# Two layers of a streaming encoder on one core: the sixteen products of o(t) in another order

## The reference, cut to what matters

```python
def step(S, inp):
    qb, kb, vb, gb = (t.astype(f32) for t in inp)
    b = jnp.cumsum(gb, axis=1)
    inter = jnp.einsum('bthk,bhkv->bthv', qb * jnp.exp(b), S)
    decay = jnp.exp(jnp.where(causal, b[:, :, None] - b[:, None, :], -jnp.inf))
    att = jnp.einsum('bthk,bshk,btshk->bhts', qb, kb, decay)
    intra = jnp.einsum('bhts,bshv->bthv', att, vb)
    b_end = b[:, -1]
    S_new = jnp.exp(b_end)[..., None] * S + jnp.einsum(
        'bshk,bshv->bhkv', kb * jnp.exp(b_end[:, None] - b), vb)
    return S_new, inter + intra
```

## Time and profile before

| | |
|---|---|
| median of 3 runs | 2413.31 us (2410.1 to 2415.28) |
| the profiled execution | 2407.27 us |
| its span, first to last instruction | 2405.3 us |
| TensorE busy in the span | 2186.8 us (91%) |
| mean granted TensorE clock | 0.939 of full speed |
| TensorE's share of the chain that ended last | 27% of the pieces the page prints |
| L1083 and L1085 in that chain | 1.3% each |

### The profile page before, as it was taken

The page is one execution under the profiler, slowest core; times in us unless marked ns, Lnnn a source line. Parts: engine busy times, 40 slices in busy tenths (PEclk is TensorE's granted clock), DMA queues, the critical chain, the costliest instruction groups (busy, mean ns, idle before and its releaser), DMA issues. The chain is left out here.

```text
span 2405.3 us, 27372 instructions
## 1 busy us (share of the span) xinstructions
PE 2186.8 (91%) x9906; PEld 1331.1 (55%) x9930; DVE 1484.6 (62%) x3125; ACT 643.1 (27%) x1478; POOL 328.1 (14%) x418
## 2 busy tenths in 40 slices
PE   4999999997999968889959999999989999789887
PEld 3544444466777755545445444444667677545554
DVE  3357999995545454654333589999955454564651
ACT  3333001113333323232143420010133333233331
POOL 0000000000000043543200000000000001353541
PEclk9999999998999968998979999999989999698988
DMA  7111322213022020221051113222120220111211
GB/s 276 63 65 62 114 73 72 66 39 69 12 81 76 1 96 22 90 87 62 36 174 49 64 67 110 72 76 66 42 62 7 82 75 31 66 64 49 97 53 55
DMA packets 144006, 169.95 MB, mean 71 GB/s; under 512 B 68560, under 2 KB 106192, under 8 KB 143600
## 3 DMA queue, kind: packets, MB, share of 16 engines
q1 hardware_dynamic: 118400, 135.52, 17.6%
q10 hardware_dynamic: 25472, 32.66, 3.8%
HBM read 115.53 MB, written 62.50 MB: 74 GB/s over the span
## 5 line engine op out<-in xcount | busy, mean ns | idle before, releaser
L767 PE MATMUL ps<-wring,xnT_arena 128*128 128x512 f32 (+3 forms) x2304 | 883.0, 540 | 0.0
L767 PEld LDWEIGHTS ps<-wring,xnT_arena 128*128 128x128 f32 x2304 | 430.7, 190 | 431.4 <-issue 369.4
L1483 DVE TENSOR_SCALAR_CACHE_REDUCE arena<-arena,theta 32x1056 bf16<-32x1056 f32 x496 | 471.6, 987 | 8.8
L1065 PE MATMUL ps<-arena 128*128 128x128 f32 (+1 forms) x632 | 134.4, 343 | 100.2 <-DVE arena L1671 84.3
L1571 DVE TENSOR_REDUCE small<-ps 128x1 f32<-128x192 f32 (+9 forms) x148 | 114.1, 771 | 154.9 <-PE ps L942 148.3
L1065 PEld LDWEIGHTS ps<-arena 128*128 128x128 f32 x632 | 103.1, 213 | 188.6 <-DVE arena L1671 142.8
L1009 PE MATMUL ps<-wring,arena 128*128 128x512 f32 x320 | 172.8, 662 | 5.7 <-DVE arena L1612 5.7
L1176 ACT COPY arena<-ps 128x512 f32<-128x512 f32 (+2 forms) x96 | 51.2, 533 | 464.4 <-PE ps L767 464.4
L1468 DVE SCALAR_TENSOR_TENSOR arena<-arena,iw 128x512 f32<-128x512 f32 (+6 forms) x224 | 135.7, 606 | 57.3 <-ACT arena L1231 50.4
L1324 ACT ACTIVATE arena<-ps,small 128x192 f32<-128x192 f32 (+9 forms) x148 | 111.0, 750 | 159.5 <-DVE small L1571 159.4
L1009 PE MATMUL ps<-wring,xnT_arena 128*128 128x512 f32 x256 | 135.1, 652 | 0.0
(11 more groups left out here) (239 smaller groups left out, 2670.7 us busy)
## 6 DMA issues: line engine op xcount, KB each, us to landing
wring<-in_w_in SPq DMA_DIRECT2D x24, 1024.0 KB, 7.7
projected<-arena ACTq DMA_DIRECT2D x96, 256.0 KB, 2.0
arena<-residual SPq DMA_DIRECT2D x36, 512.0 KB, 5.6
arena<-projected SPq DMA_DIRECT2D x36, 384.0 KB, 3.8
arena<-projected SPq DMA_DIRECT2D x18, 512.0 KB, 5.9
residual<-arena SPq DMA_DIRECT2D x18, 512.0 KB, 2.7
wring<-in_w_out SPq DMA_DIRECT2D x8, 1024.0 KB, 6.5
out<-arena SPq DMA_DIRECT2D x16, 512.0 KB, 3.9
```

The source lines that it names most:

```text
L767: o = mm(bank(pbank(k), 0, wide), xnT[:, c, t * P:(t + 1) * P], w, start=(c == 0), stop=(c == CH - 1))
L1065: o = mm(bank(level_bank(k), 2 * n_ * g, 2 * n_), keys[:, g * P:(g + 1) * P], queries[:, :, g, :], start=True, stop=True)
L1483: V.tensor_scalar(cmp_out[r, (i % 2) * WMAX:(i % 2) * WMAX + uw[u]], score[u][r], th_, 0.0, op, ALU.add, accum_out=into[r, i:i + 1]).then_ ...
```

## The change

The products and their addresses stay the same, sixteen in each tile. Before, each head's attention product was followed by its state product. Now all eight attention products come first, then all eight state products. Among these, even and odd heads alternate, so that the weights' rows alternate between 0 to 63 and 64 to 127, and the output between banks 6 and 7. Before, each attention product had `start=True`, the flag with which a product overwrites. Now the flag stands on the first product into each bank alone (m = 0, h = 0 and 1); the other attention products have `start=False`.

```diff
-                        for m, att, vv, qb, st in ((0, attA, la[:, 2, :], QbA, s_hgrn), (1, attD, ld[:, 2, :], QbD, s_ret)):
+                        sides = ((0, attA, la[:, 2, :], QbA, s_hgrn), (1, attD, ld[:, 2, :], QbD, s_ret))
+                        n_ = NS if t == 0 else P
+                        for m, att, vv, qb, st in sides:
+                            for h in range(H):
+                                oc = (6 + h % 2) * 512 + P * m + HD * (h // 2)
+                                mm(ps[:, oc:oc + HD], att[:, h, :], vv[:, HD * h:HD * h + HD], start=(m == 0 and h < 2), stop=False, skip_group_check=True)
+                        for m, att, vv, qb, st in sides:
                             for h in range(H):
                                 a, b = hp(h)
                                 oc = (6 + h % 2) * 512 + P * m + HD * (h // 2)
-                                o = mm(ps[:, oc:oc + HD], att[:, h, :], vv[:, HD * h:HD * h + HD], start=True, stop=False, skip_group_check=True)
-                                n_ = NS if t == 0 else P
                                 o = mm(ps[0:n_, oc:oc + HD], qb[a:b, (h // 2) * P:(h // 2) * P + n_], st[a:b, 0 if t == 0 else 1, h // 2, :],
-                                       start=False, stop=True, skip_group_check=True)
+                                       start=False, stop=(m == 1 and h >= 2), skip_group_check=True)
                         o.then_inc(x_o, 1)
```

## The result

| | before | changed |
|---|---|---|
| median of the runs (4 each) | 2412.91 us (2410.1 to 2415.28) | 2311.99 us (2307.53 to 2312.84) |
| the profiled execution | 2407.27 us | 2312.26 us |
| its span | 2405.3 us | 2310.3 us |
| mean granted TensorE clock | 0.939 | 0.957 |

The changed kernel takes 0.9585 of the time before (95% interval 0.9568 to 0.9601): 100.9 us less by the medians. Forecast were 2314.7 us, and 98.6 us less. A later set of runs of the changed kernel, on another chip, gave 0.9584 (0.9557 to 0.9612; label r_changed).

A forecast was written before the change was run, and what follows sets the result against it. TensorE, waiting for nobody in tile 2, was taken as the bound. Savings of 70.9 + 11.7 + 6.0 + 10 = 98.6 us from 2413.3 gave a median of 2314.7 us; 8-in-10 range 2300 to 2350 us.

The forecast's parts named there:

- o(t) at full clock, 2.98 us: o(t): attention run 1.80 us, state products 0.90, and a change of weights at 0.14 after each.
- the rate of L979: Attention products in o(t): sixteen records in one run at the softmax stage's spacing, 0.1125 us each, 1.80 us.
- L819's strips: State products in o(t): row halves run two at a time, as four 32-row strips ran together; 0.90 us.
- Rival (c): o(t)'s attention records: same-row weight loads don't overlap running products, 3.12 us for 1.80, kernel 2338 us; chance 0.03.
- The clock: Tiles 2 to 8: TensorE's granted clock holds at 1.00 from o(t) to the next L1030, against mean 0.77.
- rival (a): Tiles 2 to 8: the clock falls all the same, 6.7 us at half clock each; 46 saved, 2367 us; chance 0.12.
- Tiles 2 to 7: Stretch from o(t) to the next L1030: 8.74 us against 14.65, 5.91 saved, twelve times, 70.9 us.
- Tile 8: Stretch from o(t) with 32 records of L1009: 17.34 us against 23.25, saved in two layers, 11.7 us.
- Tile 0: Stretch from o(t) stays at half clock: 5.78 us against 8.76, 3.0 saved, twice, 6.0 us.
- Tile 1: Stretch from o(t), clock uncertain: between 2.0 and 7.5 us saved; the middle taken, 5 each, 10 in all.
- What is late next: L1009 behind o(t) also waits for `x_zr`, ready 3.45 us after o(t)'s first record; TensorE gets there after 3.58.
- one more spell of half clock between the levels in some tiles: Levels between tiles: possible extra half clock, counted only in the forecast's own upper limit of 2325 us.

The follow-up runs named there:

- e7: Kernel before, with three added dense 128x512 products, result unused, in each o(t) from tile 1 on; 2406.52 us, ratio 0.9971.
- e3: Kernel before, reordered to two attention products, then their two state products, four times over, flags as before; 2331.45 us, ratio 0.9683.
- e9: Changed kernel with the odd heads' state products taken from rows 0 to 63 too, so no upper half; 2337.21 us.
- e1: Changed kernel with state products of all even heads first, then all odd heads, so neighbours share a half of the rows; 2320.67 us, ratio 0.9634.
- e5: Changed kernel without the eight state products in tiles 2 to 8, all waits kept; 2304.69 us.
- e4: Kernel before, with six dense output projection products (L1009) moved from behind L1093 to between the halves of o(t); 2407.06 us, ratio 0.9993.

## Why the prediction was right

**What bounds the stage.** TensorE alone did, in tiles 2 to 8; when it needed less, the end moved with it. That held.

**o(t) at full clock, 2.98 us.** The timeline of tile 4, layer 2:

```profile
2133.36 1.89 PE L1084 MATMUL ps<-arena,xnT_arena 128*128 128x64 f32 x16
2135.19 0.66 PE L1089 MATMUL ps<-s_hgrn,xnT_arena 64*128 64x64 f32 x8
2135.68 0.61 PE L1089 MATMUL ps<-s_ret,xnT_arena 64*128 64x64 f32 x8
2136.23 0.69 PE L1097 MATMUL ps<-arena,xnT_arena 128*64 128x64 f32 x16
2136.84 5.42 PE L1009 MATMUL ps<-wring,xnT_arena 128*128 128x512 f32 x12
2142.09 0.27 PE L1030 MATMUL ps<-cf,xnT_arena 128*128 128x128 f32 x1
```

By the starts of these rows: attention 1.83 us (forecast 1.80 + 0.14), state 1.04 (0.90 + 0.14), together 2.87. L1097 takes 0.61 (0.60), L1009 5.25 (5.16). The sum is 8.73 against 8.74; it comes out that close by luck, because L1009's twelve records together are 0.09 longer than forecast and the first change, from L1009 to L1084, both of 128 rows, costs nothing. The two rates behind it held record by record: attention records stand 0.112 us apart, the rate of L979, and state records start in pairs 7 ns apart, a pair every 0.112 us (0.16 after the first), the step that L819's strips had suggested. (By its own two rows, 2.29 and 2.07 us, the prediction's step would be 0.11 and not 0.1125, which takes 0.04 us from sixteen records.)

**Rival (c).** L1084's weight loads are of the same 128 rows one after the other and take about 0.2 us each, as L979's did; yet the records stand 0.112 us apart, so these loads run beside the product before. The sentence of the Trainium skill (TensorE: Matmul & The Clock Gate, Part 3: Packing small matmuls) that a load overlaps with matmuls in flight only where the row group differs does not hold for them here.

**The clock.** The choice that mattered most, and it held: 1.00 in all of tiles 2 to 8, so rival (a) is out. (The prediction has the clock of before at 1.00 for the first 3.65 us of tile 2 and at 0.50 from there. The next window of the earlier trace rows has 0.73: it fell some 1.2 us later, about 4.9 us into o(t).) Why it held is narrowed, not settled. e7 shows that the old order with dense products spread through it keeps 1.00 too; e3 and e9, both with longer o(t) (3.7 us) than the change, lose it in some tiles (two and six of the twelve); e1, with 3.4, loses it in none; but e5, with 1.8 and then a wait, lost it in one. So a change of weights does not by itself bring the fall, and without dense products in it a longer o(t) lost the clock more often; by what exactly it falls these runs do not settle. Rival (a) was nearer than its 0.12 suggests: at 3.7 us it would have been partly right.

**Tile by tile.** Tiles 2 to 7 saved 175.82 - 104.98 = 70.8 us (70.9 forecast). Tile 8 saved 11.8 (11.7). Tile 0 saved 6.3 (6.0). Tile 1 saved 7.5 in layer 1 and 5.8 in layer 2 (5 each taken, as the middle of 2.0 to 7.5): this was the mis-sized term, by 3.3 us.

**What is late next.** In tile 2, `x_zr` comes at 2071.18 + 1.28 = 2072.46, by DVE's read of the banks, and L1009 starts at 2072.6, about 0.1 us later than its place in the other tiles (8.83 for 8.73): below the 0.2 us foretold. e5 shows that it would be the bound at once.

**What the sum left out.** It has no term for the stretches outside its windows, and these took 7.2 us back, by three more spells of half clock in the levels, a longer one behind tile 0, and one stretch in which DVE took longer. The prediction had "one more spell of half clock between the levels in some tiles" in its range, and said that the levels' ACT and DVE chain is only moved: in thirteen of the fourteen stretches the chain is, but the clock across it is not. This and the tile 1 term lean opposite ways (+7.2 and -3.3 us); with 102.2 - 7.2 = 95.0 the profiled execution lies 3.6 us above its forecast of 2308.7, while the median lies 2.7 below. That the second is so is luck with the executions: the profiled one was faster than the four runs of before in the table, and the second slowest of the four after.

## What to carry to other kernels

Where small products of two kinds alternate on TensorE, try sorting them: each change between full-height and half-height weights cost 0.145 us here, more than a record of 64 columns (0.112), and half-height products on alternate halves of the rows ran two at a time. Read the granted clock by stretch before and after, since half of this gain was clock; then look for the emptiest stretch that is left and move work into it rather than around it, because a change that saves time in one place can lose the clock in another. A term for the clock outside the edited stretch belongs into the sum, not only into the range.

## What was not expected of the hardware

- Products on the other half of the rows start ahead of up to three earlier records of the first half (e1: 2112.86 beside 2112.97 and later). The Trainium skill says in TensorE: Matmul & The Clock Gate, Part 3: Packing small matmuls, that matmuls start in program order; this trace shows starts out of that order where the rows differ. It does not tell in which order they end.
- A change of kind costs the same in both directions: from the last attention record to the first state record 0.205 us, from the last state record to L1097's first 0.20, where records of a kind follow at 0.112. The step behind it is longer too, 0.16 us. Over 0.112 the two are 0.09 and 0.05, together the 0.14 that a change cost in e3. The Trainium skill has the engine drain at a change of tiling mode, without a price (TensorEngine Tiling (Array Packing), Key Properties); the longer steps of this trace agree with it.
- Work can be free: 2.63 us of added dense products in each of sixteen tiles left the kernel before where it was (0.9971), because TensorE then kept 2.4 GHz through the windows of tiles 2 to 7. The half clock that the alternating products cost hardly shrank when dense work was only moved (e4: from one o(t) to the next 6.8 us in the mean against 7.4).
